# Two layers of a hybrid attention and mixture-of-experts trunk on one core: norm chains placed beside projections, the first block of each input projection taken row tile by row tile, modulation chunks and accumulator clears at other places

## What is computed

```python
for layer in range(2):
    sh1, sc1, g1, sh2, sc2, g2 = split(silu(c) @ w_mod[layer] + b_mod[layer], 6)   # for c and c_ctx
    h = rms_norm(x, norm1[layer]) * (1 + sc1) + sh1
    if layer == 0:       # chunk gating (u, va) beside attention with q/k RMSNorm and rotary
        u, va, q, k, v = split(h @ ev_w_in)
        o = concat(chunk_gating(u, va), attention(rope(rms(q)), rope(rms(k)), v)) @ ev_w_out
    else:                # latent attention (cq, ckv, krope) beside a gated short convolution (gb, gc, hv)
        cq, ckv, kr, gb, gc, hv = split(h @ od_w_in)
        o = concat(mla(rms(cq) @ w_uq, rms(ckv) @ w_ukv, kr), gb * conv(gc * hv)) @ od_w_out
    x = x + g1 * o
    h = rms_norm(x, norm2[layer]) * (1 + sc2) + sh2
    x = x + g2 * moe(h)          # top 64 latent and 16 context tokens of each of 16 experts
return rms_norm(x, final_norm), new keys, values and latents
```

## Time and profile before

| | us |
|---|---|
| median of 3 runs | 1618.15 (1605.16 to 1621.01) |
| profiled execution, own time | 1612.83 |
| span of its trace | 1611.0 |

### The profile page before, as it was taken

One profiled execution on the slowest core, in us unless ns is written; L12 is line 12 of the kernel. 1 busy time (PEld: TensorE's weight loads), 2 busy tenths in 40 slices (PEclk: granted clock), 3 DMA queues, 4 the chain that ended last, 5 costly groups with the idle time before them and its releaser, 6 DMA issues.

```text
span 1611.0 us, 18612 instructions
## 1 busy us (share of the span) xinstructions
PE 1356.2 (84%) x7784; PEld 987.3 (61%) x7784; DVE 899.4 (56%) x1030; ACT 765.0 (47%) x880; POOL 160.8 (10%) x115
## 2 busy tenths in 40 slices
PE   5699836899778999989947998899998799999990
PEld 3479813679555655556536995466987565555550
DVE  2512063641566877778626333255329688878874
ACT  3411232650436777667524103355224676777762
POOL 1100000000010222211120000000000122222111
PEclk9589956999868999999978999789996899999995
DMA  7921037000268999999964113400301699999983
GB/s 244 357 81 53 2 130 263 2 1 27 105 226 299 360 359 361 350 334 371 334 204 139 58 51 118 133 27 1 105 25 78 221 350 359 364 360 368 363 284 139
DMA packets 98825, 322.36 MB, mean 200 GB/s; under 512 B 6367, under 2 KB 30126, under 8 KB 82358
## 3 DMA queue, kind: packets, MB, share of 16 engines
q1 hardware_dynamic: 86230, 278.39, 47.9%
q0 software_dynamic: 10400, 34.93, 7.9%
q10 hardware_dynamic: 2112, 7.87, 1.3%
HBM read 297.35 MB, written 23.81 MB: 199 GB/s over the span
## 4 chain that ended last, share of the span: by engine, by line
PE 53%; DVE 16%; DMA 15%; ACT 12%; issue 2%; SPq 0%; DVEq 0%; ACTq 0%
PE psum L750 51%; DMA stage<-in_moe_w_gate 8%; DVE w_lo L1585 7%; ACT w_hi L1499 4%; ACT arena L1431 3%; DMA stage<-in_moe_w_up 3%; DVE arena L1838 2%; DVE arena L1620 2%; DVE h_lo L1627 1%; DMA stage<-in_w_mod 1%; DMA arena<-acc_dram 1%; ACT arena L1522 1%; DMA acc_dram<-arena 1%; DMA small<-in_b_mod 1%; DMA stage<-in_ev_w_in 1%
## 5 line engine op out<-in xcount | busy, mean ns | idle before, releaser
L1585 DVE TENSOR_TENSOR w_lo<-stage,w_hi 128x2048 fp32r<-128x2048 f32 x216 | 491.8, 2281 | 211.7 <-ACT w_hi L1499 140.4
L1499 ACT ACTIVATE w_hi<-stage 128x2048 fp32r<-128x2048 f32 x192 | 366.9, 1913 | 129.3 <-DMA stage<-in_moe_w_gate 57.9
L750 PE MATMUL psum<-w_hi,h_hi 128*80 128x512 f32 (+1 forms) x848 | 334.8, 395 | 58.4 <-DVE w_lo L1585 36.7
L750 PE MATMUL psum<-w_lo,h_hi 128*80 128x512 f32 (+1 forms) x848 | 328.4, 387 | 0.0
L750 PE MATMUL psum<-w_hi,h_lo 128*80 128x512 f32 (+1 forms) x848 | 327.8, 387 | 0.0
L750 PEld LDWEIGHTS psum<-w_hi,h_hi 128*80 128x80 f32 (+1 forms) x848 | 131.7, 155 | 142.0 <-DVE w_lo L1585 41.5
L750 PE MATMUL psum<-h_hi,w_hi 128*128 128x320 f32 x672 | 211.1, 314 | 6.0 <-DVE h_lo L1627 3.5
L750 PE MATMUL psum<-h_lo,w_hi 128*128 128x320 f32 x672 | 209.7, 312 | 0.0
L750 PE MATMUL psum<-h_hi,w_lo 128*128 128x320 f32 x672 | 209.6, 312 | 0.0
L750 PEld LDWEIGHTS psum<-w_hi,h_lo 128*80 128x80 f32 (+1 forms) x848 | 132.0, 156 | 63.9 <-issue 1.8
L750 PEld LDWEIGHTS psum<-w_lo,h_hi 128*80 128x80 f32 (+1 forms) x848 | 132.3, 156 | 53.5 <-issue 1.6
...
## 6 DMA issues: line engine op xcount, KB each, us to landing
...
```

The source lines that it names most:

```text
L750: return pe.matmul(o, w, x, start=first, stop=last, skip_group_check=True)
L1499: nc.scalar.activation(split_slot(w_hi, q0), stage[:, PIECE * (p0 % SLOTS):PIECE * (p0 % SLOTS) + PIECE], ACT.Copy)\
L1585: return nc.vector.tensor_tensor(dst, src, hi.bitcast(F32), ALU.subtract)
```

## The change

Six things change.

1. Layer 0's `va`: all tokens of one row tile are multiplied as soon as this tile of `h` is ready, for the first weight block too; three PSUM names are open at once. Layer 1 takes cq first, in the same way (`project_by_rows`), and ckv and kr after it.
2. Layer 0 computes q, k and v before u. The four names of u stand between the links of the q/k norm: u0, turns of v, u1, sums, u2, spread of the root, u3, rotary. Layer 1's norms of cq and ckv stand beside gc, hv and gb in the same way.
3. The sums of q and k go to 10 rows (two heads of five tiles, `pick`), the root and the Newton step work on 10x640 numbers, and five small products (`qk spread`) bring it back to 128 partitions.
4. Modulation chunks: layer 0 makes 4 and 5 before its attention (before: 4 to 9), 6 and 7 after the output projection, 8 and 9 after the second norm's sums, 10 and 11 while that norm is applied, 12 to 14 beside the top-k. Layer 1 makes 18 and 19 before its attention (before: 18 to 22), 20 and 21 after the sums, 22 and 23 while the norm is applied. The layer-1 `x out` copies of ScalarE follow the whole norm.
5. A chunk is turned by four transposes, and VectorE reduces 4 partial rows; before, `group_pick` did that in the product.
6. The accumulators are cleared by two DMAs from a repeated 128x512 tile once the first attention output of layer 0 is there; before, ten DMAs after the first norm.

```diff
-MOD_AT = {"start": [0, 1, 2, 3], "qk": [4, 5, 6, 7], "roped": [8, 9], (0, "norm"): [10, 11], (0, "soft"): [12], (0, "top"): [13, 14],
-          "acc": [15, 16], "next norm": [17], "cq": [18, 19], "ckv": [20, 21], "kr": [22], (1, "norm"): [23], (1, "soft"): [],
-          (1, "top"): []}
+MOD_AT = {"start": [0, 1, 2, 3], "qk": [4, 5], (0, "out"): [6, 7], (0, "norm"): [8, 9], (0, "apply"): [10, 11], (0, "soft"): [],
+          (0, "top"): [12, 13, 14], "acc": [15, 16], "next norm": [17], "cq": [18, 19], (1, "out"): [], (1, "norm"): [20, 21],
+          (1, "apply"): [22, 23], (1, "soft"): [], (1, "top"): []}
+IN = {0: [("va", 512), ("va", 768), ("q", 1024), ("q", 1280), ("kv", 1536), ("u", 0), ("u", 256)],
+      1: [("cq", 0), ("ckv", 256), ("gc", 928), ("gc", 1184), ("hv", 1440), ("hv", 1696), ("gb", 416), ("gb", 672)]}
...
-            out(0), out(1), out(2), mod("qk"), mod("roped"), out(3)
+            out(0), out(1), mod("qk"), out(2), out(3)
         else:
-            mod("cq"), mod("ckv"), mod("kr"), out(0), out(1)
+            out(0), out(1), mod("cq")
...
-            pool.wait_ge(zeroed, 1)
-            for L in range(LAYERS):
-                for t in range(NT):
-                    pool.dma_start(acc_dram[L][P * t:P * t + P, :], zeros).then_inc(zero_out, 16)
-            pool.wait_ge(zero_out, 16 * LAYERS * NT)
             pool.dma_start(vtok_e[:, 0, :].rearrange("p (g d) -> p g d", g=KV),
                            a["cache_attn_v"][0, 0].rearrange("g s d -> s g d")).then_inc(cache_v_in, 16)
+
+            def clear(L):
+                pool.dma_start(acc_dram[L].rearrange("(p t) (b n) -> p (t b) n", p=P, b=2),
+                               zeros.rearrange("p (o n) -> p o n", o=1).to_broadcast([P, 2 * NT, D // 2])).then_inc(zero_out, 16)
...
+                    filled(pool, (L, "O", 0))
+                    pool.wait_ge(zeroed, 1)
+                    for layer in range(LAYERS):
+                        clear(layer)
+                    pool.wait_ge(zero_out, 16 * LAYERS)
...
+            def head_sums(name):
+
+                begin(name)
+                for m in range(5):
+                    squared[0] += 1
+                    pe.wait_ge(sq_ready, squared[0])
+                    mm(bank(name, 0)[0:10, :], pick[:, m, :], sq[m % 2][:, LAT], m == 0, m == 4)
+                    ins = mm(bank(name, 1)[0:10, 0:NC], pick[:, m, :], sq[m % 2][:, CTX], m == 0, m == 4)
+                    ins.then_inc(sq_used if m < 4 else psum_full, 1)
...
-                    ins = mm(bank(("mod turned", c))[:, 2 * b:2 * b + 2], mrow[:, P * b:P * b + P], group_pick, True, True)
+                    ins = pe.transpose(bank(("mod turned", c))[:, P * b:P * b + P], mrow[:, P * b:P * b + P], ident)
...
+            def project_by_rows(key, names, h0):
+
+                hi, lo = weights(key)
+                for name in names:
+                    begin(name)
+                for k in range(KD):
+                    h_tile(h0 + k + 1)
+                    for name, c in zip(names, (0, P)):
+                        for half in range(2):
+                            tk = slice(HT * half, HT * half + HT)
+                            ins = passes(bank(name, half)[:, 0:HT], (hi[:, k, c:c + P], lo[:, k, c:c + P]),
+                                         (h_hi[:, k, tk], h_lo[:, k, tk]), k == 0, k == KD - 1)
+                        if k == KD - 1:
+                            ins.then_inc(psum_full, 1)
...
-                        for b, tiles in enumerate(((0, 1), (2, 3), (4,))):
-                            name = ("va", j, b)
-                            begin(name)
-                            for n, t in enumerate(tiles):
-                                for k in range(KD):
-                                    h_tile(h0 + k + 1)
+                        for b in range(3):
+                            begin(("va", j, b))
+                        for k in range(KD):
+                            h_tile(h0 + k + 1)
+                            for b, tiles in enumerate(((0, 1), (2, 3), (4,))):
+                                for n, t in enumerate(tiles):
                                     tk = slice(P * t, P * t + P)
-
-                                    ins = passes(bank(name)[:, 256 * n:256 * n + 256], (h_hi[:, k, tk], h_lo[:, k, tk]),
-                                                 (hi[:, k, :], lo[:, k, :]), k == 0, k == KD - 1)
-                            ins.then_inc(psum_full, 1)
+                                    ins = passes(bank(("va", j, b))[:, 256 * n:256 * n + 256], (h_hi[:, k, tk], h_lo[:, k, tk]),
+                                                 (hi[:, k, :], lo[:, k, :]), k == 0 and n == 0, k == KD - 1)
+                                if k == KD - 1:
+                                    ins.then_inc(psum_full, 1)
...
-                    for kind in "uq":
-                        for j in range(2):
-                            project((kind, j), [(kind, 2 * j), (kind, 2 * j + 1)])
+                    for j in range(2):
+                        project(("q", j), [("q", 2 * j), ("q", 2 * j + 1)])
                     project(("kv", 0), ["k", "v"])
-
+                    project(("u", 0), [("u", 0)])
...
+                    project(("u", 0), [("u", 1)], at=(P,))
+                    head_sums("qk norm")
+                    project(("u", 1), [("u", 2)])
+                    pe.wait_ge(head_root_ready, 1)
+                    emptied(pe, "pick rows")
+                    for m in QK_ORDER:
+                        name = ("qk spread", m)
+                        begin(name)
+                        mm(bank(name, 0), pick_rows[:, P * m:P * m + P], head_root[:, LAT], True, True)
+                        mm(bank(name, 1)[:, 0:NC], pick_rows[:, P * m:P * m + P], head_root[:, CTX], True, True).then_inc(psum_full, 1)
+                    project(("u", 1), [("u", 3)], at=(P,))
                     pe.wait_ge(cs_in, 16)
...
-                    for kind in ("gc", "hv", "gb"):
-                        for j in range(2):
-                            project((kind, j), [(kind, 2 * j), (kind, 2 * j + 1)], h0=h0)
-                    project(("cq", 0), [("cq", 0), ("cq", 1)])
+                    project_by_rows(("cq", 0), [("cq", 0), ("cq", 1)], h0)
                     project(("ckv", 0), ["ckv", "kr"])
...
+                    project(("gc", 0), [("gc", 0)])
                     norm_sums("cq norm", ones_d, 2)
                     norm_sums("ckv norm", ones_d, 1, at=2)
-                    modulation("cq")
+                    project(("gc", 0), [("gc", 1)], at=(P,))
                     pe.wait_ge(cs_in, 16 * 5)
                     pe.wait_ge(perm_ready, 1)
                     emptied(pe, "kr")
                     begin("kr rot")
                     mm(bank("kr rot"), perm_odd, kr[:, P:P + NL], True, True).then_inc(psum_full, 1)
-                    pe.wait_ge(proj_norm, 6)
+                    project(("gc", 1), [("gc", 2), ("gc", 3)])
+                    for kind in ("hv", "gb"):
+                        for j in range(2):
+                            project((kind, j), [(kind, 2 * j), (kind, 2 * j + 1)])
+                    modulation("cq")
+                    pe.wait_ge(proj_norm, 1)
...
+                modulation((L, "out"))
                 norm_sums((L, "norm", 1), ones_d)
                 modulation((L, "norm"))
+                modulation((L, "apply"))
...
-                    if which == 1 and k == 3:
-                        modulation((L, "norm"), slice(1, None))
-                    if (L, which) == (LAYERS - 1, 1) and k < NT:
-                        evacuate(("x out", k), x_out[k], pair(("x out", k), n=D))
+                    if which == 1 and k in (2, 5):
+                        modulation((L, "apply"), slice(0, 1) if k == 2 else slice(1, 2))
+                if (L, which) == (LAYERS - 1, 1):
+                    for t in range(NT):
+                        evacuate(("x out", t), x_out[t], pair(("x out", t), n=D))
...
-                if (L, which) == (LAYERS - 1, 1):
+                if which == 1:
                     modulation((L, "norm"))
                 for k in range(KD + 1):
+                    if which == 1 and k in (4, 7):
+                        modulation((L, "apply"), slice(0, 1) if k == 4 else slice(1, 2))
...
+                freeing(nc.vector.tensor_reduce(new, groups, AX.X, ALU.add))
+                emptied(dve, name)
+                bias = bcol[:, nb * c:nb * c + nb].rearrange("p (b o) -> p b o", o=1).to_broadcast([P, nb, 2])
+                then(nc.vector.tensor_tensor(new, new, bias, ALU.add))
...
+                    filled(dve, "qk norm")
+                    freeing(nc.vector.tensor_scalar(head_var, pair("qk norm", 10), EPS, None, ALU.add))
+                    roots[0] += 1
+                    dve.wait_ge(root_done, roots[0])
+                    then(nc.vector.tensor_tensor(head_var, head_var, head_root, ALU.mult))
```

(10 more changed lines are left out.)

274 lines of the change are left out of this document (132 added, 142 removed).

## The result

The changed kernel takes 1554.24 us (median of 4 runs, 1551.20 to 1558.14) against 1617.61 for the kernel before: a ratio of 0.9624, 95% interval 0.9574 to 0.9674. The profiled execution took 1551.20 by its own time, with a span of 1549.4, so 61.6 less span than before. The prediction was 1557, in a range of 1537 to 1583.

A forecast was written before the change was run, and what follows sets the result against it. No engine's total was taken to bound the kernel; the change works on gaps between busy stretches. Terms -57.5 + 15 - 26.5 + 13.4 = -55.6 from the profiled 1612.83 gave 1557 us, range 1537 to 1583.

The forecast's parts named there:

- `va`: Layer 0's first projection: by row tile TensorE has no gap, its clock rises early, end at 91.4: -10.5 us.
- Layer 0 to attention: Layer 0 up to attention, `va` included: attention at 212.7 instead of 273.29, -60.5, less 3 taken back: -57.5 us.
- My 3 us for narrow products: Layer 0's q/k norm: narrow sums and spreads can lower TensorE's clock; 3 us taken back, a quarter of 10.1.
- granted clock 1.00 in 155 to 195: Sign for layer 0's stretch before attention: full TensorE clock from 155 to 195 us; staying at 0.50 would refute the forecast.
- Layer 0 after attention: Layer 0's second norm to gates: chunks moved out of the first gap come back here, +15 us, bounds +8 and +22.
- 11's turn waits for ScalarE's copy behind the sixth tile, at 434 + 12.5: Layer 0's second norm: chunk 11 turned from 446.5, logits end at 457.5 against 444.41: +13 us.
- Layer 1 to attention: Layer 1's projections up to attention: attention at 1012.5 against 1038.94, -26.5 us; -23 with kn as slow as before.
- Layer 1 after attention: Layer 1's second norm to logits: chunks and late ScalarE copies delay the logits' end, +13.4 us, bounds +5 and +18.
- Clears: Accumulator clearing, 15 us of DMA moved under layer 0's attention: counted 0; absence at 60 to 73 can help by up to 3.
- Rival 2: Both layers' first blocks: clock stays at half, losing 10.5 in layer 0 and 9.5 in layer 1: 1577 us; chance 0.08.
- Rival 1: Second norms of both layers: chunk pairs dearer than counted, some 7 us for three pairs: 1578 us; chance 0.15.
- Rival 4: Dense stretches (91 to 195, 874 to 972): clock falls to 1.2 GHz, +189, so 1746 us; chance 0.02.

The follow-up runs named there:

- late_bias: Changed kernel with VectorE's bias sums for chunks 10, 11 (22, 23) after the second norm's sixth and seventh tile instead of fourth and seventh: 1543.61 us, ratio 0.9572.
- va_back: Changed kernel with `va`'s first block and cq multiplied output tile by output tile again, as before the change: 1572.47 us, ratio 0.974.

## Why the prediction was right, point by point

- Start and total: forecast -55.6, measured -61.6 of span, and 1554.24 against 1557. That the times lie within 3 us is in part luck. I counted from the profiled execution, 5.3 below the median; from the median of 1618.15 the same sum gives 1562.5, and between the medians the change was worth 63.4. The steps below, and not the total, are what was right.
- `va`: forecast -10.5, measured -9.8 (end 101.9 to 92.1), and 11.1 by undoing it. The clock rose within the first block (1.00 from 65 on), as it had from 73 to 78 before. Right in mechanism and size.
- Layer 0 to attention: forecast -57.5 for the place, measured -59.7. My 3 us for narrow products was right in size and half right in place: the spreads and the name behind them lost it (7.63 instead of 5.5, 8.4 instead of 7.0, so 3.5), while the sums, which have 10 output rows and 128 input rows, lost nothing. (A quarter of the 10.1 that I had set as the bound is 2.5, not 3; the size was a guess between the bounds.) My sign "granted clock 1.00 in 155 to 195" failed for this reason: it is 1.00 to 183, 0.54 to 190 and 0.96 to 196.2. What made the place better than forecast was 2.0 of the `s` stage, which I had taken over from before as a fixed time. It is not one, so these 2.0 are luck.
- Layer 0 after attention: forecast +8.5 to the first tile, +13 to the end of the logits, +15 in all; measured +8.2, +13.3, +14.5. But the step "11's turn waits for ScalarE's copy behind the sixth tile, at 434 + 12.5" hid a wait: the turn came 15.05 after the first tile and not 12.5, since VectorE waited 3 for chunk 10's late pieces; the logits behind it ran at the higher clock (7.9 instead of 9.4) and made up for it. late_bias shows that the wait was real.
- Layer 1 to attention: forecast -26.5, measured -28.8. The first maximum came at 962.65 and not at 970, 76 us earlier than before instead of 69: of the 7 more, 2.2 and 2.3 are the two places ahead of the attentions and 2.2 `exp 0`. By undoing, 4.7 of the 28.8 are the products by row (the forecast had about 4) and 16.5 the chunks; the 7.6 left are the norms beneath the names, which no run took away alone.
- Layer 1 after attention: forecast +13.4 to the end of the logits, measured +14.5. That the logits for eight tiles run behind the last `x out` is what happened (6.46 and 7.03 in a row); the split was off, +3.0 before the first tile and +11.5 after, where the forecast had +1.3 and some +12. Here I had seen VectorE's wait at the fifth tile (+2.4; it was 2.92).
- Clears: 0, measured 0. Experts: 0; the stretches around them moved by -2.2 and +1.1. The turn by transposes, counted 0, was not undone by any run; in the traces four transposes take 1.12 us at the lower clock and 0.66 at the full one, and VectorE's reduction takes 0.19 a chunk; the eight products that turned a chunk before took 1.87 and 1.05. So TensorE got 0.4 to 0.7 us a chunk cheaper by it, which my sum put at nothing.
- Rival 2 (the rule on k tiles) fell with va_back. Rival 1 (dear pairs in the second norms) has a true core, loads one by one; its price in layer 0 was inside my +15. Rival 4 (half clock in dense stretches) did not come: the names ran at full clock but for a few microseconds behind each narrow stage (0.96 on average in 190 to 196.2). Its sum was wrong besides: layer 0 has 10 such names and not 13, so 24 names and +168.

The sum, -55.6 against -61.6 of span, was thus 6 too small: 2.2 from layer 0's first stretch, 2.3 from layer 1's, 2.2 of `exp 0`, less a little behind. The first and the last of these are within what identical instructions scatter.
